# Four output products: the first iteration with k outermost over three pieces

## The reference, cut to what matters

```python
# first block, layer 0: windowed attention (gqa), x and ctx; layer 1: differential attention (diff), x alone after the mixer
# second block, for each of two layers:
for l in range(DEPTH):
    h = _rmsnorm_2(x, ffn_pre_norm[l])
    x = x + 0.5 * _swiglu_2(h, ffn_pre_w_gate[l], ffn_pre_w_up[l], ffn_pre_w_down[l])
    h = _rmsnorm_2(x, mix_norm[l])
    if l % 2 == 0:
        x = x + _retention_dilated_mixer(h, ab_w_in[l // 2], ab_w_out[l // 2])
    else:
        x = x + _gla_mixer(h, gla_w_in[l // 2], gla_w_a2[l // 2], gla_b_a[l // 2], gla_w_out[l // 2])
    h = _rmsnorm_2(x, ffn_post_norm[l])
    x = x + 0.5 * _swiglu_2(h, ffn_post_w_gate[l], ffn_post_w_up[l], ffn_post_w_down[l])
# every mixer ends with its output product; in the retention mixer:
cat = jnp.concatenate([o_r.astype(h.dtype), o_d.astype(h.dtype)], axis=-1)   # o_r: 4 heads x 128, o_d: 8 heads x 64
return cat @ w_out                                                           # (256 x 1024) @ (1024 x 1024)
```

## Time and profile before

| what | value |
|---|---|
| median of 3 runs | 2914.0 us (2913.49 to 2915.66) |
| the profiled execution, its own time | 2915.17 us |
| its span in the profile | 2913.4 us |
| TensorE busy | 2775.9 us, 95% |
| VectorE busy | 1784.5 us, 61% |
| ScalarE busy | 1215.5 us, 42% |
| mean granted TensorE clock | 0.977 of full |
| chain that ended last | PE 89%, DVE 7%, ACT 2% |

### The profile page before, as it was taken

The page is one execution under the profiler, slowest core; times in us unless marked ns, Lnnn a source line. Parts: engine busy times, 40 slices in busy tenths (PEclk is TensorE's granted clock), DMA queues, the critical chain, the costliest instruction groups (busy, mean ns, idle before and its releaser), DMA issues.

```text
span 2913.4 us, 45246 instructions
## 1 busy us (share of the span) xinstructions
PE 2775.9 (95%) x17112; PEld 2436.6 (84%) x17112; DVE 1784.5 (61%) x2696; ACT 1215.5 (42%) x1817; POOL 202.9 (7%) x247
## 2 busy tenths in 40 slices
PE   5999989989999989999898999999989999999998
PEld 2888877668888778888776998999879999998998
DVE  6987434847874288732548654555666666667664
ACT  3333223743322243222326554554445556444553
POOL 0100010010100100001010001001100000000001
PEclk8999999999999999999999999999999999999999
DMA  6666332024664346533321565456425556653564
GB/s 262 201 191 191 105 98 81 8 73 147 215 191 123 110 149 192 174 96 100 110 83 32 164 177 170 145 181 203 129 82 179 176 178 188 181 165 100 171 179 127
DMA packets 119323, 424.26 MB, mean 146 GB/s; under 512 B 13408, under 2 KB 14448, under 8 KB 119072
## 3 DMA queue, kind: packets, MB, share of 16 engines
q1 hardware_dynamic: 98640, 351.32, 39.5%
q0 software_dynamic: 19520, 70.19, 8.1%
q10 hardware_dynamic: 1040, 1.05, 0.1%
HBM read 421.45 MB, written 1.05 MB: 145 GB/s over the span
## 4 chain that ended last, share of the span: by engine, by line
PE 89%; DVE 7%; ACT 2%; issue 1%; DMA 1%; POOL 0%; DVEq 0%; ACTq 0%; POOLq 0%
PE bank L707 28%; PE bank L709 28%; PE bank L708 28%; DVE WL L1518 1%; DVE rstd L1698 1%; ACT WH L1196 1%; DVE g_max L1798 1%; DMA xT<-in_xT 1%; PE bank L748 1%; DVE d_small L1860 1%; PE bank L833 1%; PE bank L693 0%; PE bank L934 0%; DVE tn L1708 0%; PE bank L911 0%
## 5 line engine op out<-in xcount | busy, mean ns | idle before, releaser
L707 PE MATMUL bank<-XH,WH 128*128 128x256 f32 (+1 forms) x3776 | 1232.9, 327 | 63.7 <-DVE XL L1717 44.3
L1518 DVE TENSOR_TENSOR WL<-raw,WH 128x1024 fp32r<-128x1024 f32 (+1 forms) x664 | 807.7, 1217 | 686.1 <-ACT WH L1196 682.4
L708 PE MATMUL bank<-XL,WH 128*128 128x256 f32 (+1 forms) x3776 | 1220.6, 323 | 0.0
L709 PE MATMUL bank<-XH,WL 128*128 128x256 f32 (+1 forms) x3776 | 1220.0, 323 | 0.0
L1196 ACT ACTIVATE WH<-raw 128x1024 fp32r<-128x1024 f32 (+1 forms) x664 | 682.7, 1034 | 860.3 <-PE bank L709 857.8
L707 PEld LDWEIGHTS bank<-XH,WH 128*128 128x128 f32 x3776 | 727.7, 193 | 128.4 <-issue 57.9
L708 PEld LDWEIGHTS bank<-XL,WH 128*128 128x128 f32 x3776 | 728.4, 193 | 55.4 <-issue 2.9
L709 PEld LDWEIGHTS bank<-XH,WL 128*128 128x128 f32 x3776 | 727.5, 193 | 53.6
L709 PE MATMUL bank<-HH,WL 128*128 128x256 f32 (+1 forms) x1408 | 459.3, 326 | 0.0
L708 PE MATMUL bank<-HL,WH 128*128 128x256 f32 (+1 forms) x1408 | 457.1, 325 | 0.0
L707 PE MATMUL bank<-HH,WH 128*128 128x256 f32 (+1 forms) x1408 | 453.7, 322 | 0.0
(11 more groups left out here) (305 smaller groups left out, 1571.3 us busy)
## 6 DMA issues: line engine op xcount, KB each, us to landing
a_rows<-in_ada_t POOLq DMA_DIRECT2D x124, 512.0 KB, 4.4
raw<-in_ffn_w_gate SPq DMA_DIRECT2D x88, 512.0 KB, 3.7
raw<-in_ffn_w_up SPq DMA_DIRECT2D x88, 512.0 KB, 4.4
raw<-in_ffn_w_down SPq DMA_DIRECT2D x64, 512.0 KB, 3.6
raw<-in_ffn_pre_w_gate SPq DMA_DIRECT2D x44, 512.0 KB, 3.7
raw<-in_ffn_pre_w_up SPq DMA_DIRECT2D x44, 512.0 KB, 4.2
raw<-in_ffn_post_w_gate SPq DMA_DIRECT2D x44, 512.0 KB, 3.6
raw<-in_ffn_post_w_up SPq DMA_DIRECT2D x44, 512.0 KB, 4.3
```

The lines of the kernel that those rows point to most:

```text
L707: nc.tensor.matmul(o, WH[:, j % 4, k, :], high, start=start, stop=False)
L708: nc.tensor.matmul(o, WH[:, j % 4, k, :], low, start=False, stop=False)
L709: return nc.tensor.matmul(o, WL[:, j % 4, k, :], high, start=False, stop=stop)
L1518: nc.vector.tensor_tensor(WL[:, b, 0:d, :], raw[:, b, 0:d, :], WH[:, b, 0:d, :].bitcast(F32), ALU.subtract).then_inc(split_done, 1)
```

## The change

The first iteration of the four output products is issued with k outermost: for each k-tile the nine matmuls of pieces 0, 1 and 2, into three banks. The banks are 4, 5, 1 in mixer 0, 4, 5, 6 in mixer 1, 4, 5, 0 in mixer 2 and 0, 1, 2 in mixer 3. Piece 3 and iteration 1 go through `piece` as before, without the waits for k-tiles, in banks 4 and 5. In mixer 2 the first three pieces take the k-tiles in the order 4, 5, 6, 7, 0, 1, 2, 3. VectorE reads each eviction from the bank that `res_bank` names; its program and ScalarE's are otherwise unchanged, and so is SP's.

```diff
+        self.wide = None
+        self.k_order = list(range(DT))
...
-            out_proj(w_out, t, mix_ready[m], gate)
+            g = out_proj(w_out, t, mix_ready[m], gate)
+            g.wide = ((4, 5, 1), (4, 5, 6), (4, 5, 0), (0, 1, 2))[m]
+            if m == 2:
+                g.k_order = [4, 5, 6, 7, 0, 1, 2, 3]
...
+        def res_bank(g, i, b):
+
+            if g.wide and isinstance(i, int) and i == 0 and b < 3:
+                return bank[g.wide[b]]
+            return bank[4 + d_bank(g, b)]
...
-            def three(g, j, b, k, start, stop):
+            def three(g, j, b, k, start, stop, i=None):
                 high, low = g.rhs(k + (DT * (b % 3) if g.down else 0), g.t)
-                o = (bank[4 + (b // 3 if g.down else b) % 2] if g.kind == "res" else bank[b])[:, 0:g.t]
+                o = (res_bank(g, i, b) if g.kind == "res" else bank[b])[:, 0:g.t]
...
+            def wide_pieces(g):
+
+                for n, k in enumerate(g.k_order):
+                    pe.wait_ge(*g.ready(k))
+                    for b in range(3):
+                        if n == 0:
+                            pe.wait_ge(split_done, g.p0 + b + 1)
+                            if b < 2 and g.wide[b] == 4 + b:
+                                pe.wait_ge(res_done, g.r0 + b + 1)
+                        last = three(g, b, b, k, n == 0, n == DT - 1, 0)
+                        if n == DT - 1:
+                            last.then_inc(piece_done, 1)
...
+                elif g.wide:
+                    wide_pieces(g)
+                    piece(g, 0, 3, 3, False)
                 else:
                     turn(0, True)
...
-                        src = bank[4 + d_bank(g, b)]
+                        src = res_bank(g, i, b)
```

## The result

The changed kernel takes 2923.12 us (median of 10 runs, 2918.98 to 2925.35) against 2914.43 us before (10 runs, 2913.36 to 2915.66): ratio 1.0028, 95% interval [1.002, 1.0036]. It is slower by 8.7 us. The forecast was 2918.7 us and its range ended at 2922.5. The profiled execution took 2923.46 us with a span of 2921.7, 8.3 more than before.

What follows compares the result with a forecast made beforehand. TensorE was taken to bound the GQA and differential products, the VectorE-ScalarE eviction chain retention and GLA. Terms 2.2 + 2.5 - 2.5 + 1.0 = +3.2 us, +4.7 with one clock fall: 2918.7 us, range 2912.5 to 2922.5.

Steps and rivals of the forecast that it cites:

- The waits of piece 3: Ahead of piece 3 TensorE waits for the second eviction: +2.2 us in GQA, +2.5 us in the differential product.
- hidden in retention and GLA: Piece 3's wait there, 3.3 us, was priced at 0 because its eviction comes later anyway, at the 3.454 us period.
- First evictions: First eviction of the output product: 2.5 us earlier in retention, 1.0 us later in GLA, moving the product's end.
- I take one fall, +1.5 us: One drop to half clock at the new holes before piece 3 in GQA and differential products: +1.5 us.
- a 1 to 2 us spread either way: Later holes, including those before the FFNs, meet clock changes at shifted times: total moves 1 to 2 us either way.
- The clock falls at every new place: Rival, chance 0.23: half clock at both holes before piece 3 and at retention's head, +7.5 us, 2921.5 us.
- TensorE is the bound and piece 3 doesn't wait: Rival, chance 0.04: TensorE bounds everywhere, retention and GLA products end earlier, -13.4 us, 2900.6 us.
- Nothing in its own terms: Rival, chance 0.13: losses and retention gain balance, or a shifted clock elsewhere covers them, 2914 us.
- the differential hole: Idle TensorE before piece 3 in the differential product, forecast 2.3 us; the every-place clock rival had half clock behind it.
- retention's head: Start of the retention product, where the every-place clock rival put a fall to half clock costing 1.3 us.

Runs made afterwards that it cites:

- Experiments 5: Changed kernel with piece 3 of the GQA and differential products in a bank of its own, without the wait for the second eviction: 2913.98 us.
- 6: Changed kernel with idle matmuls into a free bank ahead of piece 3 in GQA and the differential product, wait kept but hole filled: 2919.5 us.
- 1: Kernel before with the edit in the retention product alone: 2914.7 us against 2914.33, ratio 0.9998.
- 2: Kernel before with the edit in the GQA and differential products alone: 2923.14 us, ratio 1.003.
- 3: Kernel before, with ScalarE making the next weights' high part (WH) ahead of the norm's input in retention and GLA products: 2907.68 us, ratio 0.9978.
- 4: Changed kernel, with ScalarE making the next weights' high part (WH) ahead of the norm's input in retention and GLA products: 2915.31 us.
- Experiment 7: Kernel with the edit in retention alone, GLA projection's few-row matmuls (L1111, L1112) contracting over 128 rows of other data: 2911.39 us, ratio 0.9989.

## Why the prediction was wrong

**Right, by its own steps.** The waits of piece 3: 2.3 us in GQA (forecast +2.2), 2.6 in the differential product (+2.5), hidden in retention and GLA behind the 3.45 us period, with a bracket of 3.4 us each (3.3 named). First evictions: -2.5 in retention and +0.9 in GLA (forecast -2.5 and +1.0). Together +3.3 us against +3.2. Experiments 5 and 6 show the waits as cause, 1 and 2 that each part costs by itself what it costs in the whole, 3 and 4 that TensorE is not the bound of the last two products.

**The term that failed: the clock.** "I take one fall, +1.5 us". The one fall that I counted came, behind GQA's hole, at 1.6 us. But what is left for the clock as a whole is the measured +8.3 less 3.3 = +5.0, or +6.2 without the -1.2 at the start, which the change didn't make. Its pieces: +1.6 behind GQA's hole (3.9 less 2.3) and -0.3 in the mixer ahead of it, +2.0 in the norms and FFNs behind it, +0.4 and +0.9 around the differential product, -1.4 at the head of the GEMM behind retention, +3.0 in GLA's projection. Half-clock stretches are shown above at 618, behind the norm and in GLA's projection; that the +0.4 and the +0.9 are the clock too is concluded from what is left. The step that failed is the one that put unedited code at nothing but a 1 to 2 us spread either way: one place alone moved the total by 3, and the pieces add up to a loss. There are two reasons for it.

- I looked for falls only at brackets. GLA's projection has none: the clock fell while TensorE was 100% busy in the records, on matmuls over 16 rows and 1 row. Experiment 7 shows it.
- The trace of before is one draw of the placement, and at GLA's projection a lucky one: of the twelve later profiles nine pay between 0.9 and 4.6 us there, three pay nothing. A shift in either direction could hardly gain at that place. The forecast treated it as equally likely either way. Since the clock's places differ between executions too, the one profile of before that the forecast rests on couldn't show this.

**The rivals.** "The clock falls at every new place" gave 2921.5, close to the result, but by the wrong places: the differential hole of 2.24 us didn't fall, nor did retention's head. "TensorE is the bound and piece 3 doesn't wait" is refuted. "Nothing in its own terms" as well, though experiment 1 alone looks just like it: -3.9 and +3.0.

**What stays open.** A start 4.2 us earlier costs nothing and one 4.9 us earlier meets a fall: the start against before is the wrong measure. In the table the fall goes with the distance from the clock's own last change, and a few tenths of a us decide (404.1 falls, 404.5 doesn't). Why these distances fall and others don't isn't shown. That distance isn't the program's alone: the clock's early changes differ between executions of the same code. No kernel was profiled twice, and the ten runs of the changed kernel spread over 6.4 us, so how much of each kernel's offset is its edit and how much the execution stays open. For the same reason I can't say beforehand where another kernel's shift would fall.

## What to carry to other kernels

Interleaving pieces makes them finish together: the evictions behind them bunch up, and the next piece waits unless it has a bank of its own (then the piece after it may: 1.1 us in the differential product). Before reordering a product's matmuls, ask whether TensorE or the eviction chain sets its end; if it is the chain, only the first eviction and the period count, so finish piece 0 first and take work out of the chain (here the place of one ScalarE instruction was worth 6.7 us). In this kernel a gain or loss below about 5 us is not read off the total, nor off one profile: compare the offsets of the same instruction along the program, and list where the granted clock is at half in both traces, ahead of the few-row matmuls as well as behind the brackets.

## What the runs showed of the hardware

- The granted clock fell to half with TensorE busy for 1.99 to 2.00 of every 2 us, behind 512-column matmuls contracting over 16 rows and 1 row; over 128 rows, at the same distance from the clock's last change (420.8 us, among five kernels from 420.5 to 421.3 that fell), it didn't.
- Where the clock changes differs between executions: in unedited code at the start of the program the half clock lasts 17.1 us in five profiles and 13.7 in eight.
- Brackets of 1.99, 2.23 and 2.30 us went with half clock, brackets of 2.24 and 2.22 us did not. The length of a hole alone doesn't decide. The Trainium skill (TensorE: Matmul & The Clock Gate, section "Why this matters for your kernels") advises against idle gaps above about 3 us; here shorter ones, and none at all, did it.
- Two delays of 1.6 and 3.2 us, put in at the same place, ended in the same total, since the clock came back at the same moment in both.
- GpSimd's 128x256 addition beside VectorE's 128x1024 subtraction goes with a stretch of one of the two: 0.73 to 1.81 us, or 1.22 to 1.77 us.
